# Splits of weights, keys and decode queries moved by one or two units inside a head pair of a one-core decoder step

## What is computed

```python
q = jnp.einsum("btd,de->bte", h, p["w_q"][j]).reshape(bsz, t, N_HEADS, HEAD_DIM)
s = jnp.einsum("bqhd,bkhd->bhqk", q_blk, k, preferred_element_type=jnp.float32) * scale
s = s + fq_blk[..., :, None] - fk_t[:, :, None, :]
s = jnp.where(mask, s, -jnp.inf)
pr = jax.nn.softmax(s, axis=-1)
return jnp.einsum("bhqk,bkhd->bqhd", pr.astype(v.dtype), v)
```

## Time and profile before

| what | value |
|---|---|
| median of 3 runs | 2786.46 us |
| the profiled execution, its own time | 2786.68 us |
| its span | 2784.9 us |
| TensorE busy | 2722.1 us, 98% of the span |
| VectorE busy | 1396.5 us, 50% |
| ScalarE busy | 840.0 us, 30% |
| GpSimd busy | 120.2 us, 4% |
| mean granted TensorE clock | 0.987 of full speed |

### The profile page before, as it was taken

The page is one execution under the profiler, slowest core; times in us unless marked ns, Lnnn a source line. Parts: engine busy times, 40 slices in busy tenths (PEclk is TensorE's granted clock), DMA queues, the critical chain, the costliest instruction groups (busy, mean ns, idle before and its releaser), DMA issues.

```text
span 2784.9 us, 40986 instructions
## 1 busy us (share of the span) xinstructions
PE 2722.1 (98%) x16951; PEld 2655.4 (95%) x16951; DVE 1396.5 (50%) x1947; ACT 840.0 (30%) x1270; POOL 120.2 (4%) x82
## 2 busy tenths in 40 slices
PE   8999999999999999999999999889999999999998
PEld 8999999999999999988888999789999999999998
DVE  6876354244245245357666666655542442442444
ACT  6765311111111012334444444443211110111121
POOL 1000100000000000310000000001000000000000
PEclk9999999999999999999999999899999999999999
DMA  3113111111111111132223233111111111111112
GB/s 135 40 39 105 44 46 45 49 46 45 49 46 39 54 46 39 54 100 89 86 79 96 87 98 100 54 46 39 54 37 56 46 37 57 41 42 56 40 44 80
DMA packets 91331, 166.32 MB, mean 60 GB/s; under 512 B 18066, under 2 KB 55154, under 8 KB 91026
## 3 DMA queue, kind: packets, MB, share of 16 engines
q1 hardware_dynamic: 91154, 163.72, 19.2%
HBM read 141.60 MB, written 13.70 MB: 56 GB/s over the span
## 4 chain that ended last, share of the span: by engine, by line
PE 86%; DVE 7%; ACT 3%; issue 3%; DMA 0%; DVEq 0%; SPq 0%; ACTq 0%
PE psum L385 73%; PE psum L1142 3%; PE psum L1249 2%; DVE SB L1709 2%; DVE PTL L1727 1%; PE psum L1230 1%; PE psum L1216 1%; PE psum L1189 1%; PE psum L1171 1%; ACT PTH L951 1%; DVE SB L1719 1%; ACT SB L928 1%; DVE QHL L1659 0%; DVE X L1686 0%; DVE X L1836 0%
## 5 line engine op out<-in xcount | busy, mean ns | idle before, releaser
L367 ACT ACTIVATE WH<-WR 128x1024 fp32r<-128x1024 f32 (+2 forms) x217 | 215.3, 992 | 1034.7 <-PE psum L385 1021.1
L385 PE MATMUL psum<-XH,WH 128*128 128x352 f32 x2400 | 519.5, 324 | 1.9 <-issue 1.9
L385 PE MATMUL psum<-XH,WL 128*128 128x352 f32 x2400 | 517.2, 323 | 0.0
L385 PE MATMUL psum<-XL,WH 128*128 128x352 f32 x2400 | 516.7, 323 | 0.0
L385 PEld LDWEIGHTS psum<-XH,WL 128*128 128x128 f32 x2400 | 410.3, 187 | 1.6
L385 PEld LDWEIGHTS psum<-XH,WH 128*128 128x128 f32 x2400 | 406.8, 188 | 4.1 <-issue 2.5
L385 PEld LDWEIGHTS psum<-XL,WH 128*128 128x128 f32 x2400 | 405.7, 187 | 1.6
L1568 DVE TENSOR_TENSOR X<-psum,X 128x1056 f32<-128x1056 f32 x63 | 79.2, 1258 | 371.2 <-PE psum L385 371.2
L376 DVE TENSOR_TENSOR WL<-WR,WH 128x1024 fp32r<-128x1024 f32 (+2 forms) x217 | 245.9, 1133 | 9.5 <-ACT WH L367 9.5
L385 PE MATMUL psum<-FYH,WH 128*128 128x352 f32 x1134 | 245.3, 324 | 0.0
L385 PE MATMUL psum<-FYH,WL 128*128 128x352 f32 x1134 | 244.4, 323 | 0.0
(11 more groups left out here) (255 smaller groups left out, 3822.0 us busy)
## 6 DMA issues: line engine op xcount, KB each, us to landing
WR<-in_wfi SPq DMA_DIRECT2D x96, 512.0 KB, 3.5
WR<-in_wfo SPq DMA_DIRECT2D x64, 384.0 KB, 3.0
WR<-in_wa SPq DMA_DIRECT2D x24, 512.0 KB, 3.6
WR<-in_wqkv SPq DMA_DIRECT2D x24, 512.0 KB, 4.0
X<-in_xT SPq DMA_DIRECT2D x16, 528.0 KB, 6.0
CC<-in_ck SPq DMA_DIRECT2D x128, 64.0 KB, 1.9
CC<-in_cv SPq DMA_DIRECT2D x128, 64.0 KB, 1.9
out_k<-KS SPq DMA_DIRECT2D x8, 528.0 KB, 2.7
```

Source lines behind the costliest of these rows:

```text
L367: nc.scalar.activation(WH[:, par, 0:n], WR[:, par, 0:n], ACT.Copy).then_inc(w_hi, 1)
L385: mm = nc.tensor.matmul(psum[0:m, 3 * slot + c, 0:CH], w, x[:, k, c * CH:(c + 1) * CH], start=(k == 0 and part == 0), stop=(k == nk - 1 an ...
```

## The change

Nothing is added or removed. Inside a head pair, the first low and high split of the V weights goes from unit 7 (VectorE) and unit 6 (ScalarE) one unit up, the key split of the second head goes from unit 6 to unit 4 on both engines, the decode queries' copies go from unit 11 to 12, and the low key split of the next pair's first head from unit 15 to 16 (its high part stays in 15).

```diff
-HI_SLOTS = [1, 6, 13]
-LO_SLOTS = [2, 7, 14]
+HI_SLOTS = [1, 5, 13]
+LO_SLOTS = [2, 6, 14]
 Q_SLOT, K_SLOT = 10, 15
...
                 for v in range(UNITS + 3):
                     if v == (2 if c == NHP - 1 else 1):
                         queries_hi(c, t, 1)
-                    if v == (3 if c == NHP - 1 else 6):
+                    if v == (3 if c == NHP - 1 else 4):
                         keys_hi(c, t, 1)
...
                         chunk_in(c, t, (3, 5, 8).index(v), QS)
-                    if v == 6:
+                    if v == 4:
                         keys_lo(c, t, 1)
...
                         queries_lo(c + 1, t, 0)
-                    if v == Q_SLOT + 1:
+                    if v == Q_SLOT + 2:
                         decode_queries(c + 1, t)
-                    if v == K_SLOT:
+                    if v == K_SLOT + 1:
                         keys_lo(c + 1, t, 0)
```

## The result

The changed kernel takes 2796.94 us (median of 10 runs, 2794.15 to 2798.63), the kernel before 2788.01 us in the same comparison (10 runs, 2786.32 to 2790.73). The ratio is 1.0029, 95% interval 1.002 to 1.0039: slower by 8.9 us. The forecast was slower, 2792.3 us, that is 5.6 us above the profiled execution of before (2786.68 us).

What follows compares the result with a forecast made beforehand. TensorE, busy 98% of the span, was taken as the bound, with its waits resting on latency through ScalarE. 2786.68 us plus 5.6 for the weight split, all else 0, gave 2792.3; range 2785.5 to 2798.

Steps and rivals of the forecast that it cites:

- VectorE's load in units 7, 11 and 15 is not the bound: PTL there waits for ScalarE's PTH by 0.29, 0.80 and 0.29 us, so taking splits out was worth 0.
- The weight split in unit 6 waits for step 24 and moves all behind it: Unit 6: VectorE's low part starts 0.49 to 0.92 us later per pair, delaying unit 8's product; 5.6 us over seven pairs.
- The moves to units 4, 12 and 16 cost nothing, with their cover: Idle time in these units covers the moved splits and copies; worth 0, unit 16 having the thinnest cover.
- The clock adds nothing on average: Granted clock falls earlier or later in the decode product's small matmuls; plus or minus 4 us, 0 in the sum.
- the split's term: Weight split into unit 6, delaying unit 8's product in seven pairs: 5.6 us, bounds 3.4 and 6.4 us.
- The wait in units 12 and 16 stays: TensorE's waits for products in units 12 and 16 neither grow nor shrink; only unit 8's grows.
- The rival that it costs more: Unit 16's cover tears (3.5 us) or the clock falls in unit 8 (10 us and more); 2796 to 2802, 10%.
- The faster rival: Waits in units 8, 12 and 16 shrink as VectorE's load falls; at most 9.7 us, 2777 us; 8%.

Runs made afterwards that it cites:

- e1: The change with the weight split back in units 6 and 7, the other three moves kept; 2787.2 us against 2789.44 of before, ratio 0.9993.
- e5: The kernel before, but in odd units of pairs 0 to 6 ScalarE makes PTH before the copy X; 2778.16 us against 2788.96, ratio 0.9958.
- e3: The change, but VectorE's low weight split stays in unit 7; 2787.91 us, ratio 0.9995 to the kernel before.
- e10: The kernel before with one wait added: ScalarE's key split in unit 6 waits for step 24 of the projections; 2794.66 us against 2788.93, ratio 1.0023.

## Why the prediction was right or wrong

- *VectorE's load in units 7, 11 and 15 is not the bound.* Right. e1 empties these places; its median is 2.2 us lower, which is not clear of noise, and its units 7, 8 and 11 are 1.0 us shorter. e5 moves a copy on ScalarE and gains 10.8.
- *The weight split in unit 6 waits for step 24 and moves all behind it.* Right in mechanism, in place (L1142 ends ScalarE's idle time, 0.92 us) and nearly in size: 4.9 us in units 7 and 8 where the sum had 5.6. The step that was mis-sized is the 2.25 us from the split's start to PTL, taken unchanged from the earlier trace rows. It is 2.13 now (1501.95 to 1504.08), since the sum of halves follows the split sooner; 0.12 x 7 = 0.8 us, a little more than what is missing. The wait at the product of unit 8 was to be some 1.3 us and is 0.71; the rest shows in unit 7, of which the text said that a part would. e3 adds that ScalarE's own delay costs 0.7 us over the seven pairs when it stands alone, and it is covered by VectorE's in the change, as written.
- *The moves to units 4, 12 and 16 cost nothing, with their cover.* Right, e1.
- *The clock adds nothing on average.* Not contradicted: units 0 to 3 take 159.3 us in the change's profile and 159.2 before. In the other profiles they take between 154.7 and 164.0, up and down without regard to what was changed, so the 4 us either way were a fair size.
- *What failed* is what the text left out of the weight split's move. It costed the split's readers on VectorE and TensorE, and of the DMAs only those of the key split ("Its two DMAs go out sooner. Worth 0"). SP too waits for the low weight split, with the mask row behind it, and GpSimd with the weights behind that. This was 6.4 us in unit 10, less 1.7 in units 11 and 12 where the query split was freed: 4.7 us net, as much as the term that was forecast. With the 4.9 us of units 7 and 8 it makes 9.6 of the 10.0 us by which the pairs grew; the median grew by 8.9.
- *The range held by luck.* 2796.9 us lies within 2785.5 to 2798 and near the top of the forecast's own 2789 to 2797 because 4 us had been set aside for the clock, and it was GpSimd that used them; the split's term alone, at its upper bound, ends at 2786.7 + 6.4 = 2793.1. The lower end of 2789 does not follow from its terms either: 2786.7 + 3.4 - 4 is 2786.1.
- *The wait in units 12 and 16 stays.* Right (-0.2 and +0.3 us), but the sentence looked only at the waits that existed; the new one of 1.2 us is in unit 10, where there was none.
- *The rival that it costs more* (2796 to 2802) had the time right and the reason wrong: neither did unit 16 tear (77.9 against 77.6) nor did the granted clock fall in unit 8 in any pair.
- *The faster rival* was refused on the right rows, and e5 bears them out. The releaser's name in TensorE's waits was VectorE, and the engine to mend was ScalarE.

## What to carry to other kernels

When an instruction is moved up, list everyone who waits for it, the DMA queues first, and follow what each of them starts sooner: an engine that was far from the critical path may meet the one that is on it. Where GpSimd and VectorE work in the same stretch, look at the start of each against the other to a tenth of a microsecond, and tie the one with slack to a place where it meets nothing, rather than to the moment when its data happens to land. And follow a wait one step past the engine it names: here that engine was waiting for another, whose order of two instructions was worth more than all moves of splits.

## What the runs showed of the hardware

- A scaling of 128x1024 on VectorE (0.75 us alone) that starts 0.05 to 0.4 us behind GpSimd's multiplication of the same size (1.90 us alone) takes 2.40 to 2.05 us, and ends about 0.55 us after GpSimd. If it starts 0.13 us or more ahead, GpSimd takes up to 2.38 us instead. In e5 one started 0.03 us ahead by the profile and was still held up, 2.47 us long. The split with two SBUF operands (64x1024, 1.22 us alone) ends 1.1 us after GpSimd: 1.75 us in all when it started 1.23 us behind it, 2.87 us when it started 0.11 us behind (e10, pair 0). The low parts and row extremes, which read PSUM, ran beside GpSimd at their usual length (PTL of 384 columns 0.56 us, the row extreme of 896 columns 1.08 us).
- A transfer of 512 KB mostly lands later when another of 512 KB was issued shortly ahead of it: 3.9 to 4.2 us with 5.2 to 5.8 us between the two, 4.0 to 5.7 us with 1.7 to 2.2 us (pairs 0 to 4 of all twelve kernels).
